# The additions of every fourth expert row: from VectorE's one operation to GpSimd's two

## The reference

```python
def block(args):
    xt, it, gt = args
    u = expert_u[it]
    h = jax.nn.gelu(jnp.einsum('td,tkd->tk', xt, u), approximate=False)
    v = expert_v[it]
    return jnp.einsum('tk,tkd->td', gt * h, v)
```

## Time and profile before

| | us |
|---|---|
| median of 3 runs | 2121.78 (2121.22 to 2127.32) |
| the profiled execution | 2128.97 |
| its span in the trace | 2127.2 |
| GpSimd busy | 306.3 (14%), 256 gathers |
| VectorE busy | 829.6 (39%) |
| TensorE busy (matmul) | 1750.3 (82%) |
| first gather starts, last addition into x ends | 610.36, 1437.64 |

### The profile page before, as it was taken

The page is one execution under the profiler, slowest core; times in us unless marked ns, Lnnn a source line. Parts: engine busy times, 40 slices in busy tenths (PEclk is TensorE's granted clock), DMA queues, the critical chain, the costliest instruction groups (busy, mean ns, idle before and its releaser), DMA issues. The chain is left out here.

```text
span 2127.2 us, 17331 instructions
## 1 busy us (share of the span) xinstructions
PE 1750.3 (82%) x6552; PEld 1135.5 (53%) x6552; DVE 829.6 (39%) x1514; ACT 438.1 (21%) x928; POOL 306.3 (14%) x260
## 2 busy tenths in 40 slices
PE   7999997998857579899565667666999978789997
PEld 6845855665755345447222222225887465468853
DVE  2414212323365776545996656652000015410001
ACT  1041113321121344312322222222000011210000
POOL 0000000000011253331345544410000000000000
PEclk9999986988986799999779898998999999999999
DMA  4342220223532599998879999984444342134442
GB/s 185 141 172 100 95 104 0 79 79 133 211 122 99 192 419 423 400 424 353 336 270 422 421 421 422 421 346 168 158 158 151 144 184 101 62 134 158 158 158 99
DMA packets 53778, 458.60 MB, mean 216 GB/s; under 512 B 6480, under 2 KB 7120, under 8 KB 9680
## 3 DMA queue, kind: packets, MB, share of 16 engines
q0 software_dynamic: 36864, 268.45, 31.0%
q1 hardware_dynamic: 16848, 189.28, 23.4%
HBM read 456.65 MB, written 1.05 MB: 215 GB/s over the span
## 5 line engine op out<-in xcount | busy, mean ns | idle before, releaser
L385 PE MATMUL ps<-xT,panels 128*128 128x256 f32 x2048 | 446.6, 381 | 5.3 <-PEq L546 4.0
L1041 PE MATMUL ps<-main 128*128 128x512 f32 x580 | 313.2, 686 | 143.7 <-ACT main L1022 143.6
L385 PEld LDWEIGHTS ps<-xT,panels 128*128 128x128 f32 x2048 | 391.3, 191 | 60.3 <-issue 6.6
L1041 PEld LDWEIGHTS ps<-main 128*128 128x128 f32 x580 | 118.8, 217 | 322.9 <-ACT main L1022 195.7
L957 POOL DMA_INDIRECT main<-in_expert_uv,main x196 | 234.7, 1197 | 353.9 <-DVE xT L988 172.2
L975 DVE SCALAR_TENSOR_TENSOR main<-main 128x1024 f32<-128x1024 f32 x196 | 237.2, 1223 | 117.9 <-DMA main<-in_expert_uv,main 116.4
L957 POOL DMA_INDIRECT panels<-in_expert_uv,main x60 | 71.4, 1190 | 735.4 <-DVE main L1801 609.9
L2137 PE MATMUL ps<-panels,main 128*128 128x512 f32 x352 | 151.4, 592 | 0.0
L1041 PE MATMUL ps<-panels,main 128*128 128x512 f32 x188 | 101.3, 680 | 56.1 <-ACT main L1022 56.1
L419 PE MATMUL ps<-panels,xT 128*128 128x512 f32 x320 | 143.1, 600 | 1.1 <-PEq L688 1.1
L2157 DVE TENSOR_TENSOR main<-main,ps 128x512 f32 (+1 forms) x22 | 15.1, 688 | 302.2 <-PE ps L385 302.2
(11 more groups left out here) (248 smaller groups left out, 1565.2 us busy)
## 6 DMA issues: line engine op xcount, KB each, us to landing
panels<-in_wall SPq DMA_DIRECT2D x82, 2048.0 KB, 8.2
main<-in_rows SPq DMA_DIRECT2D x14, 512.0 KB, 7.7
main<-in_expert_uv,main POOLq DMA_INDIRECT x196, 19.0
main<-in_sub_keys SPq DMA_DIRECT2D x2, 1024.0 KB, 13.4
mats<-in_mats SPq DMA_DIRECT2D x1, 1088.0 KB, 10.0
x<-in_x SPq DMA_DIRECT2D x2, 512.0 KB, 4.1
main<-in_pool_m SPq DMA_DIRECT2D x1, 1024.0 KB, 4.8
main<-in_pool_w SPq DMA_DIRECT2D x1, 1024.0 KB, 7.5
```

The lines of the kernel that those rows point to most:

```text
L385: mm = pe.matmul(self.ps[:, bank, t * T:(t + 1) * T], w[:, k, c:c + P], actT[:, k, :], start=(k == 0), stop=(k == KC - 1))
L1041: mm = pe.matmul(self.c.ps[:, b, :], self.diags[self.of_pe(r) % DIAG_RING], v[:, half * HALF:(half + 1) * HALF], start=(q == 1), stop=(q = ...
```

## The change

VectorE no longer makes the additions. GpSimd makes them in two operations: the product `v = weight * v` in place (line 996 of the new file), then `y = y + v` (line 999), with a wait on a new semaphore between the two. The first slot of a tile stays one operation (line 994). They are placed in GpSimd's list directly ahead of the gather that needs the buffer: `adds(pool, end)` makes all that are due up to the slot whose buffer is taken. What is left is made behind the last gather.

```diff
@@ gpsimd
             if self.before[r] >= 0:
+                self.adds(pool, self.before[r] + 1)
                 self.wait_used(pool, self.before[r])
             pool.indirect_dma_start(
...
+        self.adds(pool, 2 * SLOTS)
+
+    def adds(self, pool, end):
+
+        for r in range(self.next_add, end, ADD_EVERY):
+            self.add(pool, r)
+            self.next_add = r + ADD_EVERY
+
     def vector(self, dve):
...
-            if r >= BEHIND and (r - BEHIND) % ADD_EVERY == 0:
-                self.add(dve, r - BEHIND)
...
-    def add(self, dve, r):
+    def add(self, pool, r):
...
-        dve.wait_ge(self.weight_made, r + 1)
+        pool.wait_ge(self.weight_made, r + 1)
...
-            dve.wait_ge(self.added, r // ADD_EVERY)
-            ins = dve.scalar_tensor_tensor(out=y, in0=v, scalar=self.weights[:, m, q:q + 1], in1=y,
-                                           op0=ALU.mult, op1=ALU.add)
-        ins.then_inc(self.added, 1)
+            pool.tensor_scalar(v, v, self.weights[:, m, q:q + 1], None, ALU.mult).then_inc(self.weighted, 1)
+            pool.wait_ge(self.added, r // ADD_EVERY)
+            pool.wait_ge(self.weighted, r // ADD_EVERY - m)
+            pool.tensor_tensor(y, y, v, ALU.add).then_inc(self.added, 1)
```

More of the change, by code:

```diff
@@ L897, in __init__ @@
         self.dotted, self.added, self.summed = sem("row_dotted"), sem("row_added"), sem("row_summed")
+        self.weighted = sem("row_weighted")
         self.gelu_made, self.weight_made, self.diag_made = sem("gelu_made"), sem("weight_made"), sem("diag_made")
@@ L913, in __init__ @@
         self.place()
+        self.next_add = 0
         self.at_engine = {"pool": 0, "dve": 0, "act": 0, "pe": 0}
@@ L981, in add @@
         y = self.y(m)
-        dve.wait_ge(self.weight_made, r + 1)
+        pool.wait_ge(self.weight_made, r + 1)
         if q == 0:
-            dve.wait_ge(self.c.panel_done.sem, FIRST[f"w_pq.{m}"] + COUNT[f"w_pq.{m}"])
-            ins = dve.tensor_scalar(y, v, self.weights[:, m, q:q + 1], None, ALU.mult)
-        else:
-            dve.wait_ge(self.added, r // ADD_EVERY)
-            ins = dve.scalar_tensor_tensor(out=y, in0=v, scalar=self.weights[:, m, q:q + 1], in1=y,
-                                           op0=ALU.mult, op1=ALU.add)
-        ins.then_inc(self.added, 1)
+            pool.wait_ge(self.c.panel_done.sem, FIRST[f"w_pq.{m}"] + COUNT[f"w_pq.{m}"])
+            pool.tensor_scalar(y, v, self.weights[:, m, q:q + 1], None, ALU.mult).then_inc(self.added, 1)
+        else:
+            pool.tensor_scalar(v, v, self.weights[:, m, q:q + 1], None, ALU.mult).then_inc(self.weighted, 1)
+            pool.wait_ge(self.added, r // ADD_EVERY)
+            pool.wait_ge(self.weighted, r // ADD_EVERY - m)
+            pool.tensor_tensor(y, y, v, ALU.add).then_inc(self.added, 1)
     def y(self, m):
```

## The result

| | before | after |
|---|---|---|
| median of 3 runs, us | 2121.78 (2121.22 to 2127.32) | 2215.37 (2210.52 to 2220.48) |
| span of the profiled execution, us | 2127.2 | 2213.6 |
| GpSimd busy, us | 306.3 | 668.3 |
| VectorE busy, us | 829.6 | 834.8 |

The ratio is 1.0426, 95% interval 1.0385 to 1.0468: slower by 94 us. The forecast was 2182 us with 2116 to 2218, so the direction and the range for 8 in 10 held, the size was 60 of 94 us, and the forecast's own narrower range, 2137 to 2212, was missed by 3 us.

What follows compares the result with a forecast made beforehand. DMA bounds the expert gathers, VectorE only the choice of tile 1; after the change GpSimd bounds tile 1. Tile 1 +55 and tile 0 +5 on 2121.78 gave 2182 us, own range 2137 to 2212, 8-in-10 range 2116 to 2218.

Steps and rivals of the forecast that it cites:

- The bound in tile 1: Tile 1's gathers: GpSimd becomes the bound instead of DMA, 11.95 us per block against 9.95; with its end +55.4 us.
- the block: Four gathers with one product-and-addition pair on GpSimd in tile 1: 9.05 us unheld plus 2.9 of holds, 11.95 us.
- holds by the dots: GpSimd operations delayed by VectorE's two-input dots: 0.72 us for each of four dots, 2.9 us a block.
- if the pair measures ... over 5 us: Sign of being wrong: GpSimd's product and addition together, forecast 3.55 us, measuring under 2 or over 5 us.
- The tail: Behind tile 1's last gather: four more pairs on GpSimd, 19.2 us, then the additions into x, ending at 1493.0.
- Tile 0: Tile 0 in all: 6 us left from its gathers, -9 and +8 in the choice of tile 1, sum 5 us.
- the 18 us taken off for the queue: Tile 0's gathers: of 24 us lateness, 18 are paid out of the DMA queue, about 6 us remain.
- the choice of tile 1: 1000 to 1107 us, choosing tile 1's experts, VectorE the bound: 9.0 us gained from additions, 8 lost to GpSimd's pairs.
- rival C: Tile 1 fits, but GpSimd's pairs shut VectorE out in the choice of tile 1: 16 us, 2138 us; chance 0.10.
- A: Rival: the holds are absorbed, tile 1 stays as it is and 9.0 us are gained: 2113 us; chance 0.12.
- B: Rival: the block comes out at 10.0 to 10.2 us and its loss cancels the gain: 2122 us; chance 0.08.
- D: Rival: every dot holds GpSimd for its full 1.23 us, block 14.0 us: 2246 us; chance 0.15.

Runs made afterwards that it cites:

- experiment 1: Changed kernel with VectorE's 256 two-input dots replaced by one-input sums of about the same length: 2141.46 us, ratio 1.008.
- experiment 4: Changed kernel with GpSimd making the additions of tile 0 only, VectorE those of tile 1: 2150.81 us, ratio 1.0132.
- experiment 7: Kernel before with every eighth slot added on VectorE instead of every fourth, TensorE summing the other seven: 2114.65 us, ratio 0.9977.
- Experiment 12: Changed kernel with every eighth slot instead of every fourth, product on ScalarE, addition on GpSimd: 2117.71 us, ratio 0.996 to the kernel before.
- the ScalarE version: Changed kernel with the product made by ScalarE and only the addition left on GpSimd: 2122.87 us, ratio 0.9987.
- the every-eighth version: Changed kernel with every eighth slot on GpSimd instead of every fourth, TensorE summing the other seven: 2125.71 us, ratio 1.0015.
- experiments 1 and 2: One-input sums in place of VectorE's dots, in the changed kernel (1: 2141.46 us) and in the kernel before (2: 2124.16 us, ratio 0.9992).

## Why the prediction was right, and where its size was off

**The bound in tile 1: right.** That GpSimd's room was 3.6 us in a block and not the idle 86% of the page held, and with it the direction. Forecast: block 11.95, gathers of tile 1 367 us. Measured: 11.86 and 366. That the block came out within 0.1 us is luck, though: the two terms behind it were wrong in opposite ways, by 1.4 us too little and by 1.5 too much:

| term of the block, us | forecast | measured |
|---|---|---|
| four gathers and their gaps | 4.96 | 4.69 |
| product and addition | 3.55 | 5.21 (2.87 + 2.34) |
| hand-offs | 0.54 | 0.42 (0.15 + 0.27) |
| unheld | 9.05 | 10.3 (10.42 in experiment 1) |
| holds by the dots | 2.9 | 1.4 |

The addition was near the forecast of 2.20 (1.8 x 1.22). The mis-sized term is the product: I took 1.8 times VectorE's 0.75 us = 1.35 and it is 2.87, 3.8 times. The memset of one element, from which the ratio came (0.106 us), says little of an operation of 2.87 us on 1024 elements, and the two engines order the forms differently: VectorE's tensor_scalar (0.75 us) is faster than its tensor_tensor (1.22), GpSimd's is slower (2.87 against 2.34). My upper end, twice VectorE's times (3.94 us), did not hold the 5.21 either. So "what doesn't fit are the holds" was wrong: the pair alone no longer fitted. By a sign that the prediction itself had named, it was wrong there: "if the pair measures ... over 5 us". It measured 5.21 us unheld and 5.68 on average. Two other signs missed as well: the DMA share was to be near 0.83 and is 0.96, and from gather to dot pass 6 to 12 us, not 6 to 9. The holds exist and cost much, but 0.36 us a dot and not 0.72. Dots that start inside a product run on at 1.23 us (rows above), and a gather that has run for 0.14 us when a dot starts is not held; that these two make the difference is argued, not shown.

The Trainium skill's GPSIMD Engine Reference, section Performance versus the Vector engine, has a ratio of 1.96 for a tensor_tensor, from which the prediction's estimate for the addition was 2.4 us; the trace has 2.34 and agrees. The Trainium skill's "SBUF — State Buffer", section Who interferes with whom, has GpSimd's reads of SBUF and VectorE's instructions with two SBUF inputs shut each other out in either order. For the addition the trace agrees in both orders (44 dots that started inside one took 2.32 us on average, 27 additions that started inside a dot 2.94). For the product it agrees in one order only: products that started inside a dot were held (3.64 us on average over 17 in the trace), while 51 dots that started inside a product took 1.37 us on average. There the measurement decides. That gathers are held, for which the prediction went by the rows, experiment 1 bears out for VectorE's tensor_tensor too.

**The tail: nearly right.** Gather 255 to the additions into x: 22.6 us by the forecast's numbers, 27.1 measured, because the pairs are longer. Missed were the 6.4 us until the next stage starts. No row of before could show it, since GpSimd ended 42 us earlier there.

**Tile 0: wrong.** Forecast +5, measured +25.7. Its first step came out near, from gather 20 to gather 55, 97.4 us forecast and 95.9 measured, against 73.1, by the same luck as the block: without the dots' holds it is 85.2 us (experiment 1), where the forecast without them was 72.0. The queue then paid back 12 of the 23 us at the dot of slot 55 (10.5 us late, 6 forecast), but only there: by the dot of slot 63 the lateness is 20 us. In experiment 4, whose lists are the same up to there, it is 19 us at slot 55 already. The step that failed is the 18 us taken off for the queue. The likely reason is that DMA is loaded until about 950 us (400 to 424 GB/s before, in the page's slices from 745 us on), so bytes not moved from 750 to 840 us have no time left to be moved in. I treated the depth of a queue as a gain that stays. In tile 1 that is right, since it ends with the queue; in tile 0 the queue has to be deep again.

Then comes the choice of tile 1, for which I had put -9 + 8. The dots are 18.8 us late at slot 80 and 24.5 at slot 127 (at slot 96, in between, 10.4, but experiment 7, with nothing but gathers on GpSimd, dips there by 9 us as well): 182.3 us in place of 176.6, +6 and not -1. In that stretch VectorE's additions, 15.4 us, are gone, but the dots take 65.2 us in place of 58.5, and its 269 other operations 92.2 in place of 75.3. The groups of the small ones among them show rival C's mechanism, in the changed kernel:

```profile
L1808 DVE SCALAR_TENSOR_TENSOR main<-main 128x32 f32<-128x32 f32 x4 | 4.4, 1107 | 0.1
L1791 DVE TENSOR_TENSOR main<-main 128x32 f32<-128x32 f32 x4 | 4.0, 992 | 0.1
L1795 DVE TENSOR_SCALAR main<-main 128x32 uint32<-128x32 uint32 x4 | 2.8, 708 | 0.0
L1816 DVE TENSOR_TENSOR main<-main,small 128x32 f32<-128x32 f32 x4 | 2.8, 702 | 0.1
```

In the kernel before:

```profile
L1799 DVE SCALAR_TENSOR_TENSOR main<-main 128x32 f32<-128x32 f32 x4 | 0.8, 192 | 0.1
L1782 DVE TENSOR_TENSOR main<-main 128x32 f32<-128x32 f32 x4 | 0.8, 192 | 0.1
L1786 DVE TENSOR_SCALAR main<-main 128x32 uint32<-128x32 uint32 x4 | 0.7, 173 | 0.0
L1807 DVE TENSOR_TENSOR main<-main,small 128x32 f32<-128x32 f32 x4 | 0.8, 192 | 0.1
```

Operations of 0.17 to 0.19 us on 32 elements take up to 1.11 us on average there. One by one the long ones are those that run beside GpSimd's pair, such as this one, inside the addition of 1022.57 to 1024.92:

```profile
1022.72 2.25 DVE L1808 SCALAR_TENSOR_TENSOR main<-main 128x32 f32<-128x32 f32 x1
```

I had priced only the dots' third of the time. Experiment 12 shows the other side: with no product on GpSimd and half the additions, VectorE's relief comes in.

**The rivals.** A (absorbed, 2113) and B (cancelled, 2122) are what the ScalarE version and the every-eighth version show, once the block is shorter; for the changed kernel they are out. C's mechanism is real and came on top of the forecast's, but it makes only 6 of tile 0's 26 us; the others are there by slot 63. D is out: its block of 14.0 was never near.

By stages, forecast +55 (tile 1 with its tail) and +5 (tile 0): 60. Measured in the traces: +58.5, +25.7, and +6.4 for the end of GpSimd's list: 90.6. The missing 30 us are tile 0 (21), that end (6) and tile 1 with its tail (3).

## What to carry to other kernels

Before work goes to an engine that looks idle, find its room between the waits in the stretch where it feeds the bound, here 3.6 us in 9.95 and not 86% of the span, and price each operation by its own form on that engine: 2.87 and 1.89 us for the same product in two forms. Check the signs that you named one by one: here the sum came out within 0.1 us of a block whose two terms were both off by some 1.5 us. GpSimd and VectorE aren't two independent engines for operands in SBUF: what VectorE is relieved of in busy time can come back as longer rows of everything else it runs. Count lateness as paid out of a queue only if the stage ends before the queue must be deep again.

## What the runs showed of the hardware

- GpSimd's tensor_scalar on 128x1024 float32 takes 2.84 us at least with the scalar from SBUF and 2.76 as a constant (2.86 and 2.80 on average unheld); its tensor_tensor takes 2.34 us with two full operands and 1.89 us with one operand broadcast. VectorE's are 0.75 and 1.22 us.
- A gather that starts inside a two-input VectorE dot lasts to 0.8 or 0.9 us after it, so one that starts in the dot's last 0.13 us is mostly not lengthened (in the kernel before 132 gathers started inside a dot and 82 were); with one-input sums in place of the dots none of the gathers that start inside a sum is (115 and 129 of them, in experiments 1 and 2). Over the 365.8 us of tile 1's gathers in the changed kernel, removing all holds gave back 46 us.
- A VectorE operation of 0.19 us (128x32, two inputs) that started inside a GpSimd addition took 2.25 us (changed kernel).
- The next stage begins no sooner than 9.34 us after GpSimd's last elementwise operation (9.34 us in six kernels), and 0.3 us after VectorE's last one if GpSimd ended 16 us or more before.
- A DMA share near 0.96 went with 368 GB/s here, and 1.01 with 422.
